# Conv mixer and squared-ReLU MLP on one core: VectorE splits the weights from the output product to the first MLP pass, the ada units get four buffers, twelve of them move into the first w2 block, and the last outer unit goes bank by bank

## What is computed

```python
mod = silu(c) @ ada_w + ada_b                  # 6 vectors of 2048
sh1, sc1, g1, sh2, sc2, g2 = split(mod, 6)
h = rms_norm(x, norm1_g) * (1 + sc1) + sh1
u = h @ w_in + b_in                            # 2048 -> 4096, halves a and gt
u = causal_depthwise_conv(a * sigmoid(gt), w_dw, 31 taps) + b_dw
u = silu(layer_norm(u, ln_g, ln_b))
x = x + g1 * (u @ w_out + b_out)               # "output product"
h = rms_norm(x, norm2_g) * (1 + sc2) + sh2
x = x + g2 * (square(relu(h @ w1)) @ w2)       # 2048 -> 8192 -> 2048
return rms_norm(x, final_g)
```

## Time and profile before

| | |
|---|---|
| median of three runs | 2128.62 us |
| the profiled execution, its time | 2129.86 us |
| its span, first to last instruction | 2128.1 us |
| mean granted TensorE clock | 0.968 |
| busy: PE / DVE / ACT / POOL | 94% / 52% / 31% / 21% |
| matmuls | 8640 |

### The profile page before, as it was taken

One profiled execution on the slowest core, in us unless ns is written; L12 is line 12 of the kernel. 1 busy time (PEld: TensorE's weight loads), 2 busy tenths in 40 slices (PEclk: granted clock), 3 DMA queues, 4 the chain that ended last, 5 costly groups with the idle time before them and its releaser, 6 DMA issues.

```text
span 2128.1 us, 22314 instructions
## 1 busy us (share of the span) xinstructions
PE 2004.2 (94%) x8640; PEld 1632.2 (77%) x8640; DVE 1097.9 (52%) x1133; ACT 667.8 (31%) x717; POOL 451.1 (21%) x197
## 2 busy tenths in 40 slices
PE   5889999888987889999999999999999999999996
PEld 2668888656766767888888888888888888888885
DVE  5959989978698984323323332332332332232243
ACT  4334545453232222232132123123213213312332
POOL 3647999923433230000000000000000000000001
PEclk8999999979998999999999999999999999999998
DMA  9962433315866572222222222222222222222212
GB/s 399 394 258 101 158 138 118 119 60 197 341 262 246 202 292 91 87 99 99 99 99 99 99 87 91 100 96 99 99 99 99 99 99 80 101 95 99 99 59 79
DMA packets 45933, 299.58 MB, mean 141 GB/s; under 512 B 4688, under 2 KB 4688, under 8 KB 10960
## 3 DMA queue, kind: packets, MB, share of 16 engines
q1 hardware_dynamic: 45904, 299.24, 37.5%
HBM read 295.03 MB, written 4.19 MB: 141 GB/s over the span
## 4 chain that ended last, share of the span: by engine, by line
PE 72%; DVE 13%; POOL 6%; issue 4%; DMA 3%; ACT 2%; SPq 0%; DVEq 0%; POOLq 0%; ACTq 0%
PE ps L313 23%; PE ps L314 23%; PE ps L315 23%; DVE adar L760 3%; POOL wlo L1055 3%; DMA adar<-ada 3%; DVE adar L772 2%; DVE raw L772 1%; POOL pacc L1094 1%; DVE hlo L766 1%; PE ps L386 1%; DVE ps L843 1%; POOL adar L1098 1%; DVE wlo L783 1%; ACT whi L472 1%
## 5 line engine op out<-in xcount | busy, mean ns | idle before, releaser
L313 PE MATMUL ps<-hhi,whi 128*128 128x512 f32 (+1 forms) x1792 | 708.6, 395 | 61.7 <-DVE hlo L766 29.8
L314 PE MATMUL ps<-hlo,whi 128*128 128x512 f32 (+1 forms) x1792 | 704.9, 393 | 0.0
L315 PE MATMUL ps<-hhi,wlo 128*128 128x512 f32 (+1 forms) x1792 | 704.4, 393 | 0.0
L472 ACT ACTIVATE whi<-raw 128x2048 fp32r<-128x2048 f32 x176 | 336.1, 1910 | 680.5 <-PE ps L315 680.5
L313 PEld LDWEIGHTS ps<-hhi,whi 128*128 128x128 f32 x1792 | 341.4, 191 | 141.0 <-issue 56.2
L313 PE MATMUL ps<-dhi,whi 128*128 128x512 f32 x1024 | 399.8, 390 | 11.7 <-DVE dlo L1020 11.7
L314 PE MATMUL ps<-dlo,whi 128*128 128x512 f32 x1024 | 399.6, 390 | 0.0
L315 PE MATMUL ps<-dhi,wlo 128*128 128x512 f32 x1024 | 399.3, 390 | 0.0
L315 PEld LDWEIGHTS ps<-hhi,wlo 128*128 128x128 f32 x1792 | 340.9, 190 | 72.2
L314 PEld LDWEIGHTS ps<-hlo,whi 128*128 128x128 f32 x1792 | 341.6, 191 | 70.7
L783 DVE TENSOR_TENSOR wlo<-raw,whi 128x2048 fp32r<-128x2048 f32 x127 | 291.0, 2292 | 95.6 <-ACT whi L472 95.6
(11 more groups left out here) (142 smaller groups left out, 951.3 us busy)
## 6 DMA issues: line engine op xcount, KB each, us to landing
raw<-w SPq DMA_DIRECT2D x176, 1024.0 KB, 4.8
adar<-ada SPq DMA_DIRECT2D x80, 1024.0 KB, 5.0
raw<-ada SPq DMA_DIRECT2D x16, 1024.0 KB, 8.5
xb<-xT SPq DMA_DIRECT2D x8, 1024.0 KB, 9.6
out<-xb SPq DMA_DIRECT2D x5, 512.0 KB, 4.3
out<-xb SPq DMA_DIRECT2D x6, 256.0 KB, 3.8
csb<-c SPq DMA_DIRECT2D x1, 1024.0 KB, 4.9
pr<-par SPq DMA_DIRECT2D x1, 368.0 KB, 14.3
```

Source lines behind the costliest of these rows:

```text
L313: pe.matmul(out, whi[:, slot, t], xhi, start=first, stop=False, skip_group_check=True)
L314: pe.matmul(out, whi[:, slot, t], xlo, start=False, stop=False, skip_group_check=True)
L315: return pe.matmul(out, wlo[:, slot, t], xhi, start=False, stop=last, skip_group_check=True)
L472: act.activation(whi[:, q % WS, :], raw_slot(q), ACT.Copy).then_inc(whi_done, 1)
```

## The change

- **VectorE instead of GpSimd** splits the low parts of units 34 to 57 (B0, B1, C0 and the first units of w2). GpSimd has nothing to do between A1 and the end.
- **Ada units** 44 to 83 go through four buffers, two in `adar` and two slots of `raw`; the weights use the other two slots of `raw` up to unit 63. 13, 16 and 10 ada units are done in B0, B1 and C0 (0 to 3 beside each weight unit, written out as a table), two at the end of the convolution as before.
- **Twelve ada units**, 84 to 95, which hold most of g2, are done by VectorE in the first w2 block, two behind each of units 58 to 63. For this c is loaded a second time, into the buffer `quad` (the former `ta`, `tb`, `sq`, `ssum`), once the first hidden values are done, and ScalarE applies silu to it again (`cs_ready` 2).
- **TensorE's order inside a unit**: it first waits for `whi` alone and does the products with whi, and waits for `wlo` only then. The count of matmuls is unchanged. In outer units it does hhi for eight banks, then hlo, then wlo.
- **The last outer unit** of A0, B0 and C0 goes bank by bank: the six matmuls of a bank together, with a signal `bank_done` after each of the first seven. ScalarE's work on bank 0 can begin while the others are still being summed. The unit waits at its start for its `wlo` and for the last `hlo`.
- The small steps that make sc2 and sh2 (L953 to L958), which stood behind the last sum of squares of B1, stand two outputs earlier.

```diff
-LO_POOL = W2_0 + 2
-
+LO_POOL = B0 + 2
 
 M_G1, M_SC2, M_SH2, M_G2 = 2 * KC, 3 * KC, 4 * KC, 5 * KC
 ADA = 6 * KC
-ADA_A1, ADA_B0, ADA_B1, ADA_C0 = 12, 17, 17, 18
-
-SH2_EARLY = KC + 2 * KC + ADA_A1 + ADA_B0 + ADA_B1 - M_G2
+ADA_A1 = 12
+ADA_B0, ADA_B1, ADA_C0 = (0, 0, 1, 1, 2, 3, 3, 3), (0, 2, 3, 3, 3, 3, 2, 0), (3, 3, 0, 2, 2, 0, 0, 0)
+ADA_B = 2 * KC + ADA_A1
+ADA_C = ADA_B + 1 + sum(ADA_B0) + sum(ADA_B1)
+G2_LATE = ADA_C + sum(ADA_C0)
+SH2_EARLY = ADA_C - M_SH2
+STREAM2 = W2_0 + BLK
...
+            def load_ada_b(a):
+                if a % 4 >= 2 and a < ADA_B + 4:
+                    sp.wait_ge(wlo_done, B0 - 3 + a % 4)
+                else:
+                    sp.wait_ge(ada_used, a - 1 if a < ADA_B + 2 else a - 3)
+                home = adar if a % 4 < 2 else raw
+                sp.dma_start(home[:, a % 4:a % 4 + 1, :], ada[:, a:a + 1, :]).then_inc(adab_in[a % 4], 16)
...
+            def load_g2(a):
+                sp.wait_ge(ada_used, a - 1)
+                sp.dma_start(raw[:, 2 + a % 2:3 + a % 2, :], ada[:, a:a + 1, :]).then_inc(g2_in[a % 2], 16)
...
+            load_unit_b(W2_0 + 3)
+            sp.wait_ge(dlo_done, BLK)
+            sp.dma_start(quad[:], c.partition_broadcast(P)).then_inc(c_in, 16)
...
-            def product(bank, slot, tile, xhi, xlo, first, last):
-
-                t = slice(tile * P, (tile + 1) * P)
-                out = ps[:, bank, :]
-                pe.matmul(out, whi[:, slot, t], xhi, start=first, stop=False, skip_group_check=True)
-                pe.matmul(out, whi[:, slot, t], xlo, start=False, stop=False, skip_group_check=True)
-                return pe.matmul(out, wlo[:, slot, t], xhi, start=False, stop=last, skip_group_check=True)
+            def high(bank, slot, tile, x, first):
+
+                return pe.matmul(ps[:, bank, :], whi[:, slot, tile * P:(tile + 1) * P], x, start=first, stop=False,
+                                 skip_group_check=True)
+
+            def low(bank, slot, tile, x, last):
+
+                return pe.matmul(ps[:, bank, :], wlo[:, slot, tile * P:(tile + 1) * P], x, start=False, stop=last,
+                                 skip_group_check=True)
 
...
             def outer_unit(q, s, h0, i=None):
 
                 i, first = (0, s == 0) if i is None else (i, False)
-                pe.wait_ge(wlo_done, 2 * i + (q + s + 1))
+                pe.wait_ge(whi_done, 2 * i + (q + s + 1))
                 for kk in range(2):
                     k = 4 * i + (2 * s + kk)
+                    pe.wait_ge(hhi_done, k + (h0 + 1))
+                    for o in range(8):
+                        high(o, s, 8 * kk + o, ch(hhi, k), first and kk == 0)
                     pe.wait_ge(hlo_done, k + (h0 + 1))
                     for o in range(8):
-                        last = product(o, s, 8 * kk + o, ch(hhi, k), ch(hlo, k), first and kk == 0, False)
+                        high(o, s, 8 * kk + o, ch(hlo, k), False)
+                    if kk == 0:
+                        pe.wait_ge(wlo_done, 2 * i + (q + s + 1))
+                    for o in range(8):
+                        last = low(o, s, 8 * kk + o, ch(hhi, k), False)
                 last.then_inc(unit_done, 1)
 
-            def outer_units(q, h0):
+            def outer_units(q, h0, order=range(8)):
                 for s in range(2):
                     outer_unit(q, s, h0)
-                with loop(ET.PE, 1, 4) as i:
+                with loop(ET.PE, 1, 3) as i:
                     for s in range(2):
                         outer_unit(q, s, h0, i)
-
-            def inner_unit(slot, bank, seen):
-
-                pe.wait_ge(wlo_done, seen)
+                outer_unit(q, 0, h0, 3)
+                pe.wait_ge(wlo_done, q + 8)
+                pe.wait_ge(hlo_done, h0 + KC)
+                for n, o in enumerate(order):
+                    for kk in range(2):
+                        k = KC - 2 + kk
+                        high(o, 1, 8 * kk + o, ch(hhi, k), False)
+                        high(o, 1, 8 * kk + o, ch(hlo, k), False)
+                        last = low(o, 1, 8 * kk + o, ch(hhi, k), kk == 1)
+                    last.then_inc(bank_done if n < 7 else unit_done, 1)
+
+            def inner_unit(slot, bank, q, off=0):
+
+                pe.wait_ge(whi_done, off + (q + 1))
                 for k in range(KC):
-                    last = product(bank, slot, k, ch(hhi, k), ch(hlo, k), k == 0, k == KC - 1)
+                    high(bank, slot, k, ch(hhi, k), k == 0)
+                    high(bank, slot, k, ch(hlo, k), False)
+                pe.wait_ge(wlo_done, off + (q + 1))
+                for k in range(KC):
+                    last = low(bank, slot, k, ch(hhi, k), k == KC - 1)
...
+            pe.wait_ge(whi_done, W2_0 + 1)
             pe.wait_ge(relu_done, 2)
             for n, k in enumerate(HIDDEN_ORDER):
+                pe.wait_ge(dhi_done, n + 1)
+                for nn in range(2):
+                    high(4 + nn, 0, 8 * nn + k, ch(dhi, k), n == 0)
+                if n == 0:
+                    pe.wait_ge(wlo_done, W2_0 + 1)
+                for nn in range(2):
+                    low(4 + nn, 0, 8 * nn + k, ch(dhi, k), False)
                 pe.wait_ge(dlo_done, n + 1)
                 for nn in range(2):
-                    last = product(4 + nn, 0, 8 * nn + k, ch(dhi, k), ch(dlo, k), n == 0, n == BLK - 1)
+                    last = high(4 + nn, 0, 8 * nn + k, ch(dlo, k), False)
...
+            for c in range(3):
+                act.wait_ge(bank_done, 2 * c + 2)
+                sigmoid(c, 2 * c + 1, c)
+            side_products(0)
             act.wait_ge(unit_done, A1)
-            for c in range(4):
-                sigmoid(c, 2 * c + 1, c)
-                if c == 0:
-                    split_hi(9)
-            side_products(0)
+            split_hi(9)
+            sigmoid(3, 7, 3)
...
-            act.wait_ge(unit_done, B1)
-            gated(0, 0)
-            gated(1, 1)
-            split_hi(B1 + 1)
-            for n in range(2, 8):
+            for n in range(8):
+                if n < 7:
+                    act.wait_ge(bank_done, 7 + n + 1)
+                else:
+                    act.wait_ge(unit_done, B1)
+                    split_hi(B1 + 1)
                 gated(n, n)
...
-            act.wait_ge(unit_done, W2_0)
             for n in range(BLK + 1):
+                if n < BLK - 1:
+                    act.wait_ge(bank_done, 14 + n + 1)
+                if n == BLK - 1:
+                    act.wait_ge(unit_done, W2_0)
...
+            act.wait_ge(c_in, 32)
+            act.activation(quad[:], quad[:], ACT.Silu).then_inc(cs_ready, 1)
+            for m in range(BLK):
+                split_hi(W2_0 + m + 2)
+            act.wait_ge(ada_used, ADA)
+            hidden_block(0)
...
-            for k in range(KC + 2):
+            dve.wait_ge(wlo_done, LO_POOL)
+            for k in range(6):
                 z(k)
-                if k % 2 and k > 3:
+            for j in range(8):
+                if j:
+                    split_lo(B0 + 1 + j)
+                    for k in range(4 * j + 2, min(4 * j + 6, KC + 2)):
+                        z(k)
+                for _ in range(ADA_B0[j]):
                     ada_reduce(a)
                     a += 1
                     if a == M_SC2:
                         gate1()
-            while a < 2 * KC + ADA_A1 + ADA_B0:
-                ada_reduce(a)
-                a += 1
+            assert a == ADA_B + 1 + sum(ADA_B0)
...
+            for n in range(8):
                 x1(n)
-                add_squares(n - 2, ss1_done, x1sq_done)
+                if n == 6:
+                    split_lo(B1 + 1)
+                if n >= 2:
+                    add_squares(n - 2, ss1_done, x1sq_done)
             add_squares(6, ss1_done, x1sq_done)
             for j in range(8):
-                for _ in range(ada_share(ADA_B1, j) - (j == 7)):
+                for _ in range(ADA_B1[j]):
                     ada_reduce(a)
                     a += 1
+                if j == 6:
+                    assert a == ADA_C
+                    dve.wait_ge(ada_used, a)
+                    dve.scalar_tensor_tensor(modb[:, M_SC2:M_SC2 + KC], mod[:, M_SC2:M_SC2 + KC], 1.0,
+                                             b1p[:, KC:2 * KC], ALU.mult, ALU.add).then_inc(small, 1)
+                    dve.tensor_tensor(modb[:, M_SH2:a], mod[:, M_SH2:a], col("ada_b", M_SH2, SH2_EARLY), ALU.add
+                                      ).then_inc(small, 1)
+                    dve.wait_ge(small, SMALL_G1 + 2)
...
+            split_lo(C0 + 1)
             dve.wait_ge(rstd_done, 4)
-            for k in range(KC + 2):
+            for k in range(6):
                 h2(k)
-                if (k in (5, 7) or k > 8) and a < ADA:
+            for j in range(8):
+                if j:
+                    split_lo(C0 + 1 + j)
+                    for k in range(4 * j + 2, min(4 * j + 6, KC + 2)):
+                        h2(k)
```

(54 more changed lines are left out.)

207 lines of the change are left out of this document (125 added, 82 removed).

## The result

The changed kernel takes **2077.69 us**, the median of 4 runs (2075.7 to 2078.49); the kernel before took 2128.65 beside it. The ratio is 0.9761, with a 95% interval of 0.9748 to 0.9775: 51 us gained, where 2073 us and 56 were forecast.

A forecast was written before the change was run, and what follows sets the result against it. TensorE was taken to lose 70.5 us from B0 through the first w2 unit, by waits, with GpSimd's splits holding up VectorE, and slow clock. Savings of 56.0 from 2129.9, less 1.2, gave 2073 us; range 2058 to 2094.

The forecast's parts named there:

- turn to B1, B1, turn to C0: From B0's end to C0's start: waits for gated, splits and the root shrink, saving 2.0 + 9.4 + 6.8 us.
- B0 and C0 with the turn to w2: Waits for GpSimd's splits and late hidden values go, with slow clock: B0 10.2, C0 7.3, turn to w2 14.3 us.
- The 14.3: Turn from C0 to w2: with moved ada units and bank by bank, waits of 10.3 + 1.4 and 2.6 slow clock go.
- The new wait at unit 41: Start of B1: ScalarE's split, behind gated(6), is ready 11.5 us after B0, a wait of about 0.6 (bounds 0 and 5).
- The turn from B1 to C0: Before C0: 5.0 us of the wait for the root go and TensorE starts 1.8 earlier on hhi, saving 6.8.
- A0 to A1: A1 starts 3.5 to 7.3 us earlier; 5.3 counted as reaching the convolution's end (bounds -1 and 7).
- The signs: Expected in the profile: B0 near 462, ada units 2.3 us, waits under 20 us, mostly B1 to C0, spacing kept.
- Transfers as the bound: Rival: loads limit ten units of B0, B1 and C0, giving 2082 to 2100 us; 0.22 together with a late engine.
- VectorE or ScalarE late in a new place: Rival: two or three new waits at unit 41, second c or B1, 2084 to 2097 us; 0.22 together with transfers.
- the second c: First w2 block: second silu(c) might hold up x2(0) and ScalarE's split of unit 58; taken as 0 (bounds 0 and 6).
- The order of matmuls: Rival: the new order runs slower in all units, 55 us at 0.2333 us spacing, cancelling the gain; slower than before 0.02.
- the change does nothing: Rival: TensorE's waits have another cause than GpSimd's port; no gain by an unknown or the matmuls' order, 0.02.

The follow-up runs named there:

- e5: Changed kernel, but the last twelve ada units stay in C0, four beside each of its last three units, without the second silu of c: 2089.85 us.
- e3: Changed kernel, but the last outer units of A0, B0 and C0 run whole like the others, ScalarE waiting for unit_done: 2081.44 us.
- e4: Changed kernel with ScalarE making unit 41's high part ahead of gated(2), right when B0 ends, not ahead of gated(7): 2074.2 us.
- e2: Changed kernel with the old order of matmuls in all units but the last outer ones and the first w2 unit: 2093.65 us.
- e1: Changed kernel, but GpSimd again makes the low parts of units 34 to 57: 2093.92 us.
- e7: Kernel of e4, with A0's last unit doing all products with chunk 14 first, then those with chunk 15 bank by bank: 2067.75 us.
- e6: Changed kernel with two buffers instead of four for ada units in B0, B1 and C0: 2100.56 us.
- e9: Kernel before, with only the low-part splits of units 34 to 57 moved from GpSimd to VectorE: 2117.27 us.

## Why the prediction was right, and where it was off

The gain in the profiled executions is 53.0 us; by stage, with the starts of units:

| | forecast | measured |
|---|---|---|
| up to B0's start | 5.3 + 0.7 | 4.2 |
| B0 | 10.2 | 12.0 |
| turn to B1, B1, turn to C0 | 2.0 + 9.4 + 6.8 | 12.2 |
| C0, turn to w2, first w2 unit | 7.3 + 14.3 | 23.8 |
| from the second w2 unit on | 0 | 0.8, behind the last matmul |

The wait of 0.9 us for `gated`, forecast in the third row, is measured in the row of B0. The sum came within 3 us of the measured gain partly by luck: 6.0 too much at the two turns and B1 and 1.8 up to B0, against 4.0 too little in the rows of B0 and C0 and the 0.8 at the end.

*B0 and C0 with the turn to w2*: right. In B0 one wait of 0.4 us is left, in C0 none. The 14.3 was of two parts that I didn't price one by one: e5 gives 12 to VectorE's order, e3 3 to bank by bank in all three stages.

*The new wait at unit 41* is the term that was mis-sized: 4.85 us and some 2 of slow clock, where I took 0.6 and wrote down 5 as the bound "if ScalarE's order stretches more". I had the chain right and its start wrong. By my sum VectorE is through with the ada units 11.1 us after the last unit of B0 began, about at its end; it was 3.9 us later than the end. The split before them began at 547.33 instead of 545.3, since the ada units of the unit before ran until then, and one of the three waited 1.36 for its load. The steps in the chain were 1.6, not 1.5. e4 shows the cause by taking ScalarE's split out of the chain. 4.3 more in the wait and 2 in the clock make about the 6.0 us by which this part of the table falls short. The turn from B1 to C0 gave 7.1 (17.9 to 10.8 us), for 6.8.

*A0 to A1*: the mechanism was right, also that the last unit starts at 136.6; it ends at 149.4. The convolution's first chain began 1.75 us later than before (161.07 for 159.32), just beyond my "1 us later", and B0 still 4.2 us earlier. With the old order (e2) the chain starts at 161.44 and B0 at 469.9, so the lead that A1 makes hangs at least in part on the order of the matmuls. In e5, e1 and e4, with the same code up to B0, B0 starts at 463.9, 461.2 and 461.1: in the changed kernel and e5 12 matmuls between 370.7 and 376.0 us go at half clock, in e1 and e4 none, and this goes with the 3 us. So my 6.0 lies inside what varies from run to run. e7 shows that the new wait for the last `hlo` cost 5 us more.

*The signs.* Those that the prediction named came, but for three: B0 begins at 464.2 instead of near 462; the turn from B1 to C0 is 7.2 of the 17.3 us of waits, not most of them; and unit 41 waits more than the 3 us by which the forecast called itself wrong.

*The rivals.* Transfers as the bound: not with four buffers, 2.0 us of waits for loads in all from B0 to C0. The Trainium skill's page "DMA: Bandwidth & Descriptors", section "Bandwidth", gives 341 GB/s for a transfer of 1 MB, from which the prediction estimated 14 us more. That rate was no bound here, with loads queued one behind the other: in 464 to 760 us of the changed kernel, in slices of 7.4 us, up to 432 GB/s were moved,

```profile
GB/s 2 0 157 129 141 143 240 203 350 426 432 424 428 334 74 82 360 358 407 426 422 344 382 391 158 0 145 45 389 133 320 249 93 49 142 142 144 120 306 198
```

and ten of the forty slices are above 380. With two buffers the loads cost 23 us (e6), by my reading not by their rate but by when they may start. VectorE or ScalarE late in a new place came true once, unit 41; the second c, at unit 58, did not: silu ran from 762.31 to 764.23, and unit 58 started at 769.57 without a wait. The order of matmuls costs nothing. That the change does nothing is refuted by the 51 us, and e1, e2, e5 and e6 show that each of four parts carries some of it.

*What I did not see* is how the parts hang together. Taken back one at a time from the changed kernel, splitter, order, buffers and ada units cost 18, 16, 23 and 12 us, 69 together where there are 51; made alone, the splitter gives 11 and the order 5. My sum gave every wait for a split to GpSimd's hold. It came out since all parts were in the change; by the same words I would have given e9 some 30 us.

Open is how much of e1's 18 us is GpSimd's hold on VectorE and how much GpSimd's own 4.6 us a split: a GpSimd working beside VectorE's splits wasn't tried. Open too is why the same wait of TensorE is followed by slow matmuls in one execution and not in another.

## What to carry to other kernels

A wait that names the splitter can be owed to four things at once: who does the work, how early its result is wanted, how early its input may be loaded, and what stands ahead of it in the list. Taking back each part of a finished change, and making one part alone, gives different sizes; only both together show that each removes the bound behind the other. When a chain of small steps alternates between two engines, look for the big step that stands in the middle of it and whose input was ready before the chain began: moving it ahead was worth 4 us here for one line. And a wait by which a stage is entered should be placed before the first product that needs the late chunk, not before the unit.
